# One more 128-column product behind each chunk's state products in an RWKV core

## The reference

```python
def rwkv7_recurrence(r, decay, k, v, a, b):
    # per head, state S (value i, key j):
    # S_t = S_{t-1} diag(w_t) + (S_{t-1} a_t) b_t^T + v_t k_t^T ;  y_t = S_t r_t
    def step(S, inp):
        r_t, w_t, k_t, v_t, a_t, b_t = inp
        sa = jnp.einsum('bhij,bhj->bhi', S, a_t)
        S = S * w_t[:, :, None, :] + sa[..., None] * b_t[:, :, None, :] + v_t[..., None] * k_t[:, :, None, :]
        y = jnp.einsum('bhij,bhj->bhi', S, r_t)
        return S, y
    ...
    _, ys = lax.scan(step, S0, xs)
```

## Time and profile before

| what | us |
|---|---|
| median of 3 runs | 2597.88 |
| the runs | 2595.58 to 2601.07 |
| the profiled execution, whole | 2603.71 |
| its span, first to last instruction | 2602.0 |
| of the span: the RWKV core, 560 to 845 | 285 |

### The profile page before, as it was taken

The page is one execution under the profiler, slowest core; times in us unless marked ns, Lnnn a source line. Parts: engine busy times, 40 slices in busy tenths (PEclk is TensorE's granted clock), DMA queues, the critical chain, the costliest instruction groups (busy, mean ns, idle before and its releaser), DMA issues.

```text
span 2602.0 us, 46767 instructions
## 1 busy us (share of the span) xinstructions
PE 2529.3 (97%) x18850; PEld 2120.8 (82%) x18850; DVE 820.0 (32%) x1269; ACT 935.1 (36%) x1556; POOL 984.5 (38%) x470
## 2 busy tenths in 40 slices
PE   8999999998888999999999999999999999999998
PEld 6888886777776788888899998888889777788887
DVE  5222015455553332210432012221043566322200
ACT  4222223634554343321433233332143565333321
POOL 4444442332222354444434444444444101444442
PEclk9999999998898999999999999999999998999999
DMA  4333231210000233322234443332232241333221
GB/s 155 97 97 97 97 105 53 78 42 4 4 4 20 82 105 97 97 97 97 97 122 139 144 142 101 97 97 94 96 118 81 66 128 52 97 96 95 96 96 62
DMA packets 181773, 230.37 MB, mean 89 GB/s; under 512 B 16408, under 2 KB 119992, under 8 KB 181624
## 3 DMA queue, kind: packets, MB, share of 16 engines
q1 hardware_dynamic: 181624, 228.20, 27.5%
HBM read 213.47 MB, written 14.68 MB: 88 GB/s over the span
## 4 chain that ended last, share of the span: by engine, by line
PE 84%; issue 11%; POOL 2%; ACT 1%; DVE 1%; DMA 0%; SPq 0%; POOLq 0%; ACTq 0%; DVEq 0%
PE bank L343 19%; PE bank L345 19%; PE bank L344 19%; PE bank L350 6%; PE bank L352 6%; PE bank L351 6%; POOL w_lo L318 2%; PE bank L1231 1%; PE bank L1344 1%; PE bank L1314 1%; PE bank L1362 1%; PE bank L1790 1%; PE bank L1546 1%; PE bank L1448 1%; PE bank L1266 0%
## 5 line engine op out<-in xcount | busy, mean ns | idle before, releaser
L318 POOL TENSOR_TENSOR w_lo<-w_raw,w_hi 128x1024 fp32r<-128x1024 f32 x376 | 905.1, 2411 | 1342.0 <-ACT w_hi L313 1341.3
L313 ACT ACTIVATE w_hi<-w_raw 128x1024 fp32r<-128x1024 f32 x376 | 395.3, 1058 | 1031.3 <-PE bank L345 861.4
L343 PE MATMUL bank<-xg_hi,w_hi 128*128 128x512 f32 x1408 | 549.7, 390 | 6.6 <-POOL w_lo L318 5.2
L344 PE MATMUL bank<-xg_lo,w_hi 128*128 128x512 f32 x1408 | 547.8, 389 | 0.0
L345 PE MATMUL bank<-xg_hi,w_lo 128*128 128x512 f32 x1408 | 547.8, 389 | 0.0
L343 PEld LDWEIGHTS bank<-xg_hi,w_hi 128*128 128x128 f32 x1408 | 264.3, 188 | 64.3 <-issue 5.4
L345 PEld LDWEIGHTS bank<-xg_hi,w_lo 128*128 128x128 f32 x1408 | 264.3, 188 | 55.4
L344 PEld LDWEIGHTS bank<-xg_lo,w_hi 128*128 128x128 f32 x1408 | 264.3, 188 | 55.3 <-issue 0.7
L343 PE MATMUL bank<-hid_hi,w_hi 128*128 (+1 forms) x704 | 274.4, 390 | 0.0
L344 PE MATMUL bank<-hid_lo,w_hi 128*128 (+1 forms) x704 | 273.9, 389 | 0.0
L345 PE MATMUL bank<-hid_hi,w_lo 128*128 (+1 forms) x704 | 273.9, 389 | 0.0
(11 more groups left out here) (287 smaller groups left out, 3111.9 us busy)
## 6 DMA issues: line engine op xcount, KB each, us to landing
w_raw<-in_ffn_w_in SPq DMA_DIRECT2D x352, 256.0 KB, 3.0
w_raw<-in_ffn_w_out SPq DMA_DIRECT2D x176, 256.0 KB, 2.8
w_raw<-in_w_kv SPq DMA_DIRECT2D x96, 256.0 KB, 3.1
w_raw<-in_rwkv_w_rkv SPq DMA_DIRECT2D x48, 256.0 KB, 2.8
w_raw<-in_attn_w_q SPq DMA_DIRECT2D x48, 256.0 KB, 3.1
k_dram<-stage SPq DMA_DIRECT2D x6, 1024.0 KB, 4.5
v_dram<-stage SPq DMA_DIRECT2D x6, 1024.0 KB, 5.5
keys<-k_dram SPq DMA_DIRECT2D x24, 256.0 KB, 3.5
```

What stands on the lines that cost most here:

```text
L313: act.activation(w_hi[:, s, :], w_raw[:, s, :], ACT.Copy).then_inc(w_hi_ready, 1)
L318: pool.tensor_tensor(w_lo[:, s, :], w_raw[:, s, :], w_hi[:, s, :].bitcast(F32), ALU.subtract).then_inc(w_lo_ready, 1)
L343: pe.matmul(o, hi, x_hi, start=start, stop=False)
L344: pe.matmul(o, hi, x_lo, start=False, stop=False)
```

## The change

A function `stream_pe` is added, and `z_pe` calls it once at its end, behind the read-out products. It issues one fp32 product with the identity as weights (128 by 128, the full array) and the same identity as its 128 columns, and writes it to columns 128 to 255 of bank 6. It waits for nothing and raises no semaphore, and no engine reads these columns.

```diff
+        def stream_pe(pe):
+
+            pe.matmul(bank[6][:, P:P + 128], ident[:, :], ident[:, 0:128], start=True, stop=True)
+
         def z_pe(pe, q, c):
             need(pe, "state", q, c)
             need(pe, "zv", q, c + 1)
@@
                 last = pe.matmul(y_bank(q)[head(1 - hh), c * CH:(c + 1) * CH], ar[head(hh), 2 - q % 3, c, 1, :],
                                  state[head(hh), c % 2, :], start=False, stop=False)
             done(last, "read_out")
+            stream_pe(pe)
```

## The result

| kernel | median us | lowest to highest | executions |
|---|---|---|---|
| before | 2596.73 | 2595.49 to 2601.07 | 4 |
| the change | 2618.06 | 2616.78 to 2620.24 | 4 |

The change makes the kernel slower: 1.0074 times, 95% interval 1.006 to 1.0087, that is 19 us. On another chip, beside the kernel before again, it was 1.0049 (1.0028 to 1.007), that is 12 us. The prediction was 2596.5 us with a range up to 2607, and the time lies above the range.

What follows compares the result with a forecast made beforehand. PE was taken as the bound, with the core's clock not always granted. Products on the path, +9.8 us, less 11.2 us from the clock made -1.4: 2596.5 us against the median; range 2587 to 2607, the forecast's own 2592 to 2603.

Steps and rivals of the forecast that it cites:

- What bounds the kernel, and where the waits are: Whole program and core: PE ends 84% of the chain; idle time ahead of the next step in chunks 1, 3, 5.
- The cover that was named: Chunks 1, 3, 5 and those without filler: idle time of 0.26 to 0.61 us hides 29 of 56 products.
- The price of one product: Core, each added product on the path: 0.33 us at full clock, between 0.23 and 0.38; 27 of them make 8.9 us.
- the term for the change of shape: Added product between products of half the rows: 0.14 to 0.15 us on top of streaming, read from changes in attention.
- The streaming, 0.23 by L2066: Two records of one added product at 0.116 us each at full clock: 0.23 us, the lower end of the price.
- 0.44 us: Price of one product by the skill's rule, 0.23 plus two unhidden weight loads of 0.107 us; not adopted.
- Chunks 4 and 6 have 16 or more products between z and u, and I take them as chunks 2 and 7: Chunks 4 and 6 of pairs 0 to 6: PE sets the time, so each added product costs the same 0.33 us.
- What low clock costs, 0.32 us per us: Core pairs: each microsecond at 1.2 GHz lengthens the time by 0.32 us, from 7.9 us over 24.5 us.
- A pair at full clock, 32.4 us from zwza to zwza: A pair at clock 1.00 throughout: 31.1 + 4 x 0.33 = 32.4 us; 31 or 33 us would fail the forecast.
- the other sign: Core's mean clock: should rise from 0.86 to about 0.92; staying at 0.86 or reaching 0.97 would fail the forecast.
- I take 35: Core: full-array work removes 35 us of low time, out of bounds 0 to 62, worth -11.2 us.
- The slower one, in which the clock doesn't answer: Core: products cost their price in chunks 2, 4, 6, 7, clock falls as often; 2608 us, 2605 to 2610; chance 0.22.

## Why the prediction was wrong

**What bounds the kernel, and where the waits are: right in the main.** The products in chunks 1, 3 and 5 gave 1.0001, those in chunks 2, 4, 6 and 7 gave 1.0048. The cover that was named holds but for 3.5 us that were put at nothing: chunk 1, chunk 3 of pairs 0 and 1, and the last pair.

**The price of one product, "I take 0.33", upper end 0.38: too small.** It measured 0.42 at full clock in chunks 2 and 7. The step that failed is the term for the change of shape. The streaming, 0.23 by L2066, was right: in the neighbours' shape the price was 0.22. The rest, put at 0.10 and at most 0.15 from the attention's changes of shape, is 0.20. It has two parts in the rows of chunk 7: the first load of weights, about 0.1 us, has nothing to run beside, and gp starts 0.205 us behind the second record, where the next record of the same shape would follow after 0.116. The row of L481 had a sign of it. The forecast divided 1.65 us by seven equal distances; in the trace the first distance is 0.37 us and the other six are 0.21 each.

The Trainium skill, "TensorE: Matmul & The Clock Gate", Part 3, The mechanism, says that weight loads overlap with running matmuls only where the row groups differ. With its load time the prediction had worked out 0.44 us and then set it aside. The run has 0.42, but the number agrees better than its working. That had both loads of the product exposed; in the trace the second starts 0.11 us behind the first, beside the first record, and what stands in its place is the wait ahead of the next shape. So the rule isn't borne out at the second load, which has the same rows as the record beside it. It is at the first, and in the version with the lower rows: ahead of gp, in the other row half, the product cost nothing (1.43 us before and 1.43 to 1.44 with it).

**"Chunks 4 and 6 have 16 or more products between z and u, and I take them as chunks 2 and 7": wrong for chunk 4.** The loss there was 0.77 us, not 0.33. The prediction had counted the fillers as work in a row. They ran abreast with z and u, and this could be read in the trace of before: 16 products, 32 records, yet u only 0.77 us behind z in pair 1. The run with chunk 4 alone confirms the place: 7.5 us for 8 products.

**The sum by places.** Chunk 2: 6 x 0.42 = 2.5. Chunk 4: 7 x 0.77 = 5.4. Chunk 7: 7 x 0.42, and 0.54 in pair 0, 3.5. Chunk 6: its distances scatter, and over pairs 0 to 6 they are 1.1 to 2.6 us above before in the three profiles with this product; I take 2. Chunk 1: 7 x 0.08 = 0.6. Chunk 3 in pairs 0 and 1, where its wait was shorter: 0.8. The last pair, at 1.2 GHz, from 0.80 to 1.14 or 1.15 in three chunks and to 1.34 in two: 2.1. Together 16.9 us, where the prediction had 9.8. Low time 103 in place of 110.6 gives back 2.1. That makes 14.8; the 12 executions of the change have 14.5 more than the 82 of before. This is a sum of full-clock prices, with one term taken from scattered values, so that the closeness is in part luck. In an execution with more of chunk 4 at 1.2 GHz the change costs more, as in the first profile.

**What low clock costs, 0.32 us per us: about right.** 0.27 over 82 executions of before; 0.40 over the 12 of the change.

**A pair at full clock, 32.4 us from zwza to zwza: too short.** The second profile of the change has three such stretches, of 32.1, 34.4 and 34.4 us; the one in the profile of before has 31.1. The core's clock stayed at 0.87 in the first profile, the other sign that was named for a forecast that fails.

**"I take 35" us of low time given back: wrong, and the larger of the two errors.** It was 8 on average over 12 executions, worth 2 us and not 11.2: 9 us of the miss, where the prices make 7. The first profile of the change has the same 79 us in the core as that of before, the one on the other chip 48. The reason given, that work of 1.6 us a pair is as large as the difference between pairs that kept the clock and pairs that lost it, took no account of the time that the product itself puts between the others. The runs agree with that from both sides, but none shows it: shape, streaming and length of the core change together in them. One column, with the obstruction and none of the streaming, has 127 us at low clock, more than before. The neighbours' shape, with the streaming and little obstruction, has 83, and three times the columns 66. So added work in the neighbours' shape gave back 28 and 47 us; the full-array product gave back 8, and why it gave so little stays open.

**The rivals.** The slower one, in which the clock doesn't answer, had the sign and nearly the mechanism, since the clock answered by 8 us; its 2608 us fell short for the two prices above.

## What to carry to other kernels

Before adding a product to a stretch of small ones, look at the shape of its neighbours (the rows and columns of the array that their weights fill), and whether records of different lines start within 0.02 us of each other: these run abreast, and a product of another shape parts them. Its price is then not only its columns but a change of shape more and the overlap that it ends. In this kernel the same columns in the neighbours' shape cost half as much where the engine sets the time, and went with less time at low clock. Even so, 24 us less at low clock with the work in the waits didn't shorten the kernel measurably. And when two kernels differ by half a percent, compare their low time before reading a price, or the absence of one, from their times.

## What the runs showed of the hardware

- A full-array fp32 product with a single column holds the next one, gp, up by 0.31 us at full clock, with 128 columns by 0.42; two 64 by 64 products of 128 columns, one in each row half, by 0.22.
- Products of one shape in different quadrants run at the same time, to 0.01 us from start to start. A product of the lower 64 rows by all columns is free ahead of one of the same shape on the upper rows (1.43 us from z to u without it, 1.43 to 1.44 with it), and holds up a 64 by 64 product on the same upper rows (1.34 us from z to u in place of 0.80, at 1.2 GHz, where two 64 by 64 products in u's own quadrants make it 0.91).
- At none of the 153 to 246 changes of shape in each of the 14 profiles does the next record start less than 0.148 us behind the last.
- In the core, PE was busy for 87% of the stretch before and 91% after, each with some 79 us at 1.2 GHz. Two single-quadrant products of 128 columns at the same places went with a mean clock of 0.92 in place of 0.86, with 384 columns with 0.96.
- Executions of one and the same kernel differ by their low time, and 0.27 us of span go with each us of it, with a correlation of 0.74; this is somewhat over half of the variance of this kernel's span.
